# A relative-bias matrix in a decoder trunk: flipped by TensorE, or read from shifted copies in DRAM

## What is computed

```python
def t5_bucket(dist):
    n = jnp.maximum(dist, 0)
    ...
    return jnp.where(n < max_exact, n, large)

bias = rel_bias[t5_bucket(dist)]          # rel_bias: 32 buckets x 8 heads
logits = jnp.einsum('bqhd,bqkhd->bqhk', qb, k_sel) * scale
logits = logits + jnp.transpose(bias, (0, 1, 3, 2))
```

## Time and profile before

| what | value |
| --- | --- |
| median of 3 runs | 1084.79 us (1084.78 to 1084.98) |
| the profiled execution: its span (its time is given in no other form) | 1083.3 us |
| PE busy | 1065.8 us, 4864 instructions |
| DVE, ACT, POOL busy | 602.3, 508.4, 33.3 us |
| DMA packets moved | 203.08 MB, 187 GB/s over the span |
| read from and written to HBM | 200.63 MB, 2.11 MB |
| mean granted TensorE clock | 0.998 of full speed (2.4 GHz) |

### The profile page before, as it was taken

One profiled execution on the slowest core, in us unless ns is written; L12 is line 12 of the kernel. 1 busy time (PEld: TensorE's weight loads), 2 busy tenths in 40 slices (PEclk: granted clock), 3 DMA queues, 4 the chain that ended last, 5 costly groups with the idle time before them and its releaser, 6 DMA issues.

```text
span 1083.3 us, 14804 instructions
## 1 busy us (share of the span) xinstructions
PE 1065.8 (98%) x4864; PEld 877.8 (81%) x4864; DVE 602.3 (56%) x719; ACT 508.4 (47%) x627; POOL 33.3 (3%) x41
## 2 busy tenths in 40 slices
PE   6999999999999999999999999999999999999996
PEld 5888788878888888888888888888888888888885
DVE  6544455544566544655555565555555566666455
ACT  7444444444454444654554454444445544444443
POOL 1000000000001300000000000000000000000004
PEclk9999999999999999999999999999999999999999
DMA  7766566666566666556556556666665555566553
GB/s 230 251 193 194 158 190 177 186 180 183 175 192 189 196 193 193 178 177 182 171 171 179 174 180 184 184 186 182 187 183 178 189 189 184 185 223 229 194 194 136
DMA packets 104841, 203.08 MB, mean 187 GB/s; under 512 B 8356, under 2 KB 8520, under 8 KB 104432
## 3 DMA queue, kind: packets, MB, share of 16 engines
q1 hardware_dynamic: 104032, 200.96, 60.8%
q0 software_dynamic: 608, 1.74, 0.5%
q10 hardware_dynamic: 176, 0.07, 0.0%
HBM read 200.63 MB, written 2.11 MB: 187 GB/s over the span
## 4 chain that ended last, share of the span: by engine, by line
PE 97%; DVE 1%; DMA 1%; ACT 0%; issue 0%; SPq 0%; ACTq 0%; DVEq 0%
PE psum L845 31%; PE psum L847 31%; PE psum L846 31%; PE psum L854 2%; DMA keep<-x 1%; DVE hl L610 0%; PE psum L948 0%; PE psum L925 0%; PE psum L974 0%; PE psum L908 0%; PE psum L924 0%; PE psum L960 0%; PE psum L959 0%; PE psum L947 0%; PE psum L958 0%; DVE keep L829 0%
## 5 line engine op out<-in xcount | busy, mean ns | idle before, releaser
L553 DVE TENSOR_TENSOR wl<-raw,wh 128x1024 fp32r<-128x1024 f32 (+1 forms) x370 | 454.3, 1229 | 437.8 <-ACT wh L339 437.7
L339 ACT CAST wh<-raw 128x1024 fp32r<-128x1024 f32 (+1 forms) x370 | 388.4, 1051 | 535.0 <-PE psum L847 532.7
L845 PE MATMUL psum<-wh,hh 128*128 128x512 f32 x1280 | 507.5, 396 | 0.0
L847 PE MATMUL psum<-wh,hl 128*128 128x512 f32 x1280 | 499.2, 390 | 0.0
L846 PE MATMUL psum<-wl,hh 128*128 128x512 f32 x1280 | 498.5, 389 | 0.0
L845 PEld LDWEIGHTS psum<-wh,hh 128*128 128x128 f32 x1280 | 240.4, 188 | 51.1 <-issue 2.9
L847 PEld LDWEIGHTS psum<-wh,hl 128*128 128x128 f32 x1280 | 240.2, 188 | 51.0
L846 PEld LDWEIGHTS psum<-wl,hh 128*128 128x128 f32 x1280 | 240.5, 188 | 48.8 <-issue 0.2
L845 PE MATMUL psum<-wh,yh 128*128 128x512 f32 x192 | 75.0, 391 | 0.0
L847 PE MATMUL psum<-wh,yl 128*128 128x512 f32 x192 | 74.7, 389 | 0.0
L846 PE MATMUL psum<-wl,yh 128*128 128x512 f32 x192 | 74.7, 389 | 0.0
(11 more groups left out here) (134 smaller groups left out, 355.6 us busy)
## 6 DMA issues: line engine op xcount, KB each, us to landing
raw<-w_in SPq DMA_DIRECT2D x288, 512.0 KB, 3.6
raw<-w_o SPq DMA_DIRECT2D x32, 512.0 KB, 3.6
raw<-p_c SPq DMA_DIRECT2D x16, 512.0 KB, 3.5
raw<-p_a SPq DMA_DIRECT2D x16, 512.0 KB, 4.1
raw<-p_b SPq DMA_DIRECT2D x16, 512.0 KB, 3.7
keep<-x SPq DMA_DIRECT2D x4, 512.0 KB, 6.0
keep<-x SPq DMA_DIRECT2D x1, 2048.0 KB, 9.5
keep<-bias_table POOLq DMA_DIRECT2D x1, 1024.0 KB, 8.1
```

The costliest lines, as they stand in the source:

```text
L339: act.copy(wh[:, slot, 0:width], raw[:, slot, 0:width]).then_inc(high_split, 1)
L553: dve.tensor_tensor(wl[:, slot, 0:width], raw[:, slot, 0:width], wh[:, slot, 0:width].bitcast(F32), ALU.subtract).then_inc(low_split, 1)
L845: pe.matmul(dst[t], h, w_h[:, j], start=start, stop=False)
L847: mm = pe.matmul(dst[t], l, w_h[:, j], start=False, stop=stop)
```

## The change

The table in DRAM becomes 128 copies of a 384-column table per head. With a row pitch of one element less than the length of a copy, partition p reads copy p from element 127 - p, so the rows come back in the right order, straight into `bias`. The flip matrix, its load, the four matmuls and the four copies go. The table is stored by four DMAs of 32 copies each, whose source is the SBUF table with a repeated (step 0) dimension. ACT waits for the stores before phase 2, in which the place of the table in SBUF is written over; POOL waits for the read instead of the copies; PE's wait for the indexer weights moves to the first transposes of phase 2.

```diff
+SKEW = 3 * P
+ROWS = 32
...
-    table_dram = nc.dram_tensor("bias_table", (HEADS, N), F32).ap()
+    table_dram = nc.dram_tensor("bias_table", (P, HEADS, SKEW), F32).ap()
...
-        onehot = early[0:BUCKETS, 0, 2560:2560 + N]
+        onehot = early[0:BUCKETS, 0, 2560:2560 + SKEW]
-        table = early[0:HEADS, 0, 3584:3584 + N]
-        flip_s = early[:, 0, 4096:4096 + P]
+        table = early[0:HEADS, 0, 3584:3584 + SKEW]
-        bias_rev = keep[:, 1, 8 * N:12 * N]
...
-            pool.dma_start(flip_s, flip).then_inc(small_loaded, 16)
...
             pool.wait_ge(table_ready, 1)
-            pool.dma_start(table_dram, table).then_inc(table_stored, 16)
-            pool.wait_ge(table_stored, 16)
-            pool.dma_start(bias_rev.rearrange("p (h s) -> p h s", h=HEADS),
-                           bass.AP(table_dram.tensor, 0, [[1, P], [N, HEADS], [1, SEQ]])).then_inc(bias_loaded, 16)
+            for i in range(P // ROWS):
+                pool.dma_start(table_dram[i * ROWS:(i + 1) * ROWS].rearrange("r h m -> h r m"),
+                               table.unsqueeze(1).to_broadcast([HEADS, ROWS, SKEW])).then_inc(table_stored, 16)
+            pool.wait_ge(table_stored, 16 * (P // ROWS))
+            pool.dma_start(bias, bass.AP(table_dram.tensor, P - 1, [[HEADS * SKEW - 1, P], [SKEW, HEADS], [1, SEQ]])
+                           ).then_inc(bias_loaded, 16)
...
-            pool.wait_ge(bias_ready, 4)
+            pool.wait_ge(bias_loaded, 16)
...
-            act.copy(table, bank[4][0:HEADS]).then_inc(table_ready, 1)
+            act.copy(table, bank[4][0:HEADS, 0:SKEW]).then_inc(table_ready, 1)
...
-            act.wait_ge(bias_done, 1)
-            for i in range(4):
-                act.copy(keep[:, 0, (8 + i) * N:(9 + i) * N], bank[i]).then_inc(bias_ready, 1)
+            act.wait_ge(table_stored, 16 * (P // ROWS))
...
-            pe.wait_ge(small_loaded, 16 * 6)
+            pe.wait_ge(small_loaded, 16 * 5)
...
-            pe.matmul(bank[4][0:HEADS], rel, onehot, start=True, stop=True).then_inc(table_done, 1)
+            pe.matmul(bank[4][0:HEADS, 0:SKEW], rel, onehot, start=True, stop=True).then_inc(table_done, 1)
...
-            pe.wait_ge(bias_loaded, 16)
-            pe.wait_ge(iw_ready, 1)
-            for i in range(4):
-                mm = pe.matmul(bank[i], flip_s, bias_rev[:, i * N:(i + 1) * N], start=True, stop=True)
-            mm.then_inc(bias_done, 1)
-
...
-                        pe.wait_ge(bias_ready, 4)
+                        pe.wait_ge(iw_ready, 1)
                         pe.wait_ge(iq_ready, c + 1)
```

More of the change, by code:

```diff
@@ L87, in trunk @@
 def trunk(nc, x, norm_g, w_in, a_ws, a_b, b_conv, p_a, p_b, p_c, w_o, rel_bias, final_g,
-          identity, flip, buckets, out):
-    table_dram = nc.dram_tensor("bias_table", (HEADS, N), F32).ap()
+          identity, buckets, out):
+    table_dram = nc.dram_tensor("bias_table", (P, HEADS, SKEW), F32).ap()
     rows = lambda w: w.rearrange("(k p) n -> p k n", p=P)
@@ L212, in trunk @@
         table_done, table_ready, table_stored = sem("table_done"), sem("table_ready"), sem("table_stored")
-        bias_loaded, bias_done, bias_ready = sem("bias_loaded"), sem("bias_done"), sem("bias_ready")
+        bias_loaded = sem("bias_loaded")
         iq_ready, iqt_done, iqt_ready = sem("iq_ready"), sem("iqt_done"), sem("iqt_ready")
@@ L1055, in _constants @@
     eye = np.eye(P, dtype=np.float32)
-    dist = np.maximum(SEQ - 1 - np.arange(N), 0)
+    dist = np.maximum(SEQ - 1 - np.arange(SKEW), 0)
     exact = BUCKETS // 2
@@ L1060, in _constants @@
     onehot = (np.arange(BUCKETS)[:, None] == bucket[None]).astype(np.float32)
-    return {"identity": eye, "flip": np.ascontiguousarray(eye[::-1]), "buckets": onehot}
+    return {"identity": eye, "buckets": onehot}
 def kernel(**inputs):
```

## The result

The changed kernel takes 1101.67 us (median of 4 runs, 1101.38 to 1102.44), the kernel before beside it 1084.88 (4 runs, 1084.78 to 1085.51): ratio 1.0153, 95% interval 1.0141 to 1.0165. The forecast was 1081.1 in a range up to 1091.0. It is slower by 16.8 us: rival one came true, with twice the stall at which it was priced (17.7 us for 9).

A forecast was written before the change was run, and what follows sets the result against it. TensorE was taken to bound the kernel, 97% of the chain; 3.44 for the flip plus 0.2 for the table's matmul, with no stall, took 1084.8 to 1081.1 us, own range 1080.6 to 1082.0, 8 in 10 up to 1091.

The forecast's parts named there:

- rival one: Early first phase, TensorE at 40 to 70 us: stores starve the weight ring, 9 us stall at T = 30, 1090 us; chance 0.33.
- The flip, 3.44 us: Between first and second phase: removing the four flip matmuls takes 3.44 us off TensorE, with no other work filling the place.
- Rival two: At the phase boundary: another wait replaces the removed pause, or T falls near 25; no change, about 1084.5 us; chance 0.10.
- The table's matmul, 0.2: TensorE's table matmul at L894 shrinks from 512 to 384 columns: 0 to 0.24 us less, taken as 0.2.
- x, 0: Kernel start: 80 KB fewer small loads on POOL's queue beside x could bring 0.24 us either way; taken as 0.
- ScalarE's new wait and POOL's list at no cost: ScalarE's wait near 113.96 us finds the table stored; POOL's issues, 2 to 4 us, make nothing late: 0 us.
- Eight partitions side by side then give 170 GB/s, T = 9 us. I take 9: T, how long the 1.57 MB of table stores occupy the DMA engines: 9 us, from the 16 KB store's packets.
- The slow end, 74: Upper bound of T, the stores' duration: eight partitions giving only their share of 340 GB/s take 74 us.
- With 2 KB for each 1.5 KB stored: Queues share engines packet for packet: loads get 2.1 MB during the stores, falling behind by T - 10.9 us.
- T - 21: TensorE's stall in us once the stores outlast the loads' share and the ring's cover; zero at T = 9.
- The cover of the ring: Prefetched weights ahead of TensorE: 3.8 us before the cast and 5.9 after, together some 10 us of lateness hidden.
- Its point of decision, T = 24.6: The stores' duration at which TensorE's stall eats the whole gain; the first stall was put at T = 21.

The follow-up runs named there:

- e5_noflip: Kernel before the change with only the flip matmuls and their copies taken out, bias rows left reversed: 1081.31 us against 1084.91.
- e4_copies32: Changed kernel storing only 32 shifted rows with one store, read back by four reads of 32 partitions: 1081.13 us, ratio 0.9964 to the kernel before.
- e3_rep2: Changed kernel with the table in two copies on 16 neighbouring partitions, each storing 64 rows instead of 128: 1087.08 us (one run).
- e1_spread8: Changed kernel with the same four stores read from eight partitions lying apart (0, 9, ... 63): 1082.73 us, ratio 0.9979 to the kernel before.
- e6_copies64: Changed kernel storing 64 shifted rows with two stores, read back by two reads of 64 partitions: 1085.46 us (one run).

## Why the prediction was wrong, step by step

- **The flip, 3.44 us: right.** e5_noflip gives 3.6 with that part alone, e4_copies32 has 3.5 left after its earlier start is taken off. Rival two, a wait in its place, is refuted by both.
- **The table's matmul, 0.2: right; x, 0: mis-sized.** The matmul gave 0.2. Together they were worth 0.84 in the profiled execution, so x gave some 0.6, beyond the 0.24 set as its bound. That bound came from bytes alone; x's landing moved by 0.6 to 2.8 us with what stood on POOL's queue (7.9 after its issue here, 8.5 before, 9.5 to 11.3 where many small pieces were added).
- **ScalarE's new wait and POOL's list at no cost: right.** POOL waited 33.0 us for the stores and ended its mask by 64.3; the bias was first used at 364.9. The stores had landed long before ScalarE came to its wait.
- **"Eight partitions side by side then give 170 GB/s, T = 9 us. I take 9": this step failed.** T was 29 to 31. The packets of a 16 KB store gave a rate for one packet, and the sum over eight partitions took for granted that they don't share a way out. They do: eight neighbours give 52 GB/s, sixteen 100, eight that lie apart 212 (the runs e3_rep2 and e1_spread8). The slow end, 74, gave each partition 340 / 128 = 2.7 GB/s; neighbours gave 52 / 8 = 6.5 each and those apart 212 / 8 = 26.5, so a partition has no such share either.
- **"With 2 KB for each 1.5 KB stored": mis-sized.** The store's packets were 4.6 KB, and the loads came through with 0.7 packets for each, 0.3 bytes per stored byte in place of 1.33. The rows read as "packet for packet" had equal shares of time, but 81 packets against 124. So the loads all but stood still, and T - 21 became T less 11 to 13: a stall of 17.7, not 8 to 10 (2.7 of it by ScalarE's list, as shown above). The cover of the ring, some 10 us, was right: the load issued at 26.98 landed after 18.5 us where 3.6 was usual, 14.9 late, and cost TensorE 4.0, so 10.9 were hidden; in e6_copies64 the load landed after 16.7 and cost 2.3, so 10.8 were.
- **The clock was left out.** About 3.0 us of low clock behind the pauses stand in no term.
- **Rival one was the mechanism,** with its place (43.7 to 65.7 us, given as 40 to 70) and its marks (ScalarE waiting for loads, TensorE for splits, stores landing over 25 us after issue: the last took 33.4). Its price of a 9 us stall was 11.7 short of the 20.7 that pauses and clock cost, from the last two points. That each engine holds a store packet while weight packets queue behind it fits the 13 to 16 store packets in flight, but no run shows the queue on an engine. Its point of decision, T = 24.6 for break-even, was too high: e6_copies64 has lost the whole gain at 14.9 (1085.5 against 1084.9).

The Trainium skill, page "SBUF — State Buffer", section "Door 1: The DMA port swizzle", was weighed and set second. Its table gives 27.6 GB/s for one port, and partitions 0 to 7 reach two, some 55 (an estimate from it); the trace agrees with 52 GB/s, and the T = 29 estimated from it with 29 to 31. For partitions 0 to 15 its table has 104 GB/s, e3_rep2 shows 100. The partitions of e1_spread8 reach eight ports by its formula, and for ranges that reach eight it measures 189 and 196; the run shows 212.

## What to carry to other kernels

Before a DMA that repeats a few rows is added beside a busy stream, price it by which partitions its source lies on, not by bytes: eight neighbours gave a quarter of the rate of eight spread ones. Then look at what such a transfer does to the others: here 52 GB/s of stores left 15 GB/s to loads that had 193, and a prefetch ring that hides some 11 us hid nothing beyond it. The cheapest cure was to store less (32 shifted rows and four reads, 1081.1 us) rather than to store the same faster; spreading the rows gave 1082.7, as the products then began 1.7 us later.

## What was not expected of the hardware

- A store's packet of 4.6 KB from partitions 0 to 7 held a DMA engine for 1.32 us, a load's of 2 KB for 0.08; the queues show engines that are 97% busy while 66 GB/s move. A full DMA share said nothing of the rate here.
- The same store issued by ScalarE came in packets of 1.5 KB, where POOL's had three rows each, and its four issues held ScalarE for 8.8 us; POOL's four took 2.7 for all (26.48 to 29.17 us). Loads felt it too: beside the stores three of five issues on SP took 3.3 to 6.5 us each, where 0.37 is usual.
- After a pause of 4 us the products ran at the lower clock from 49.2 us until the next pause at 52.4, and after one of 13.7 from 65.7 to 69.6 us (granted clock 0.50 in both), so a stall cost more than its length: about 3.0 us on 17.7.
